# Where the streamed rows and the weight rings of a two-block forward pass begin, modulo 256 bytes

## The reference, cut to what matters

```python
# first block, x: (1, 256, 2048)
z = rms_norm(h, attn_norm_g) @ w_in                      # 2048 x 5120
h = h + concat(diff_attention(...), gmlp(...)) @ w_out    # 2048 x 2048
f = rms_norm(h, ffn_norm_g)
h = h + (silu(f @ ffn_w1) * (f @ ffn_w3)) @ ffn_w2        # 2048 x 5632, twice, and back
h = h + (p @ pl_w_up) * sigmoid(h @ pl_w_gate)
x = rms_norm(h, final_norm_g)
# second block, 16 meta tokens ahead of the 256
proj = rms_norm(h, norm_mix_g) @ w_in                     # 2048 x 12288
h = h + (g_a * (pool(u) @ pool_w) * pool_scale + g_b * ((gb * conv(gc * v)) @ conv_out_w)) @ w_o
gate, up = split(rms_norm(h, norm_ffn_g) @ w_gate_up)     # 2048 x 11264
h = h + (silu(gate) * up) @ w_down
out = rms_norm(h, norm_final_g)[:, 16:]
```

## Time and profile before

| | |
|---|---|
| median of three runs | 2665.52 us |
| the profiled execution, its own time | 2665.68 us |
| its span, first to last instruction | 2663.6 us |
| TensorE busy | 2652.8 us, 15711 matmuls |
| VectorE busy | 1658.5 us |
| ScalarE busy | 1236.0 us |
| mean granted TensorE clock | 0.999 |

### The profile page before, as it was taken

The page is one execution under the profiler, slowest core; times in us unless marked ns, Lnnn a source line. Parts: engine busy times, 40 slices in busy tenths (PEclk is TensorE's granted clock), DMA queues, the critical chain, the costliest instruction groups (busy, mean ns, idle before and its releaser), DMA issues.

```text
span 2663.6 us, 39872 instructions
## 1 busy us (share of the span) xinstructions
PE 2652.8 (100%) x15711; PEld 2347.5 (88%) x15711; DVE 1658.5 (62%) x1645; ACT 1236.0 (46%) x1355; POOL 0.8 (0%) x7
## 2 busy tenths in 40 slices
PE   9999999999999999999999999999999999999998
PEld 8889888888888888888999999888888888888887
DVE  6567766555565556795676666556765645564555
ACT  5456554444444444565443443444554434443444
POOL 0000000000000000000000000000000000000000
PEclk9999999999999999999999999999999999999999
DMA  8554555655656555555555555555565555565553
GB/s 291 184 174 145 195 189 193 193 193 188 198 181 205 181 199 189 185 191 191 176 175 189 181 184 182 190 182 190 189 205 189 189 189 189 189 198 192 180 192 138
DMA packets 254251, 502.92 MB, mean 189 GB/s; under 512 B 8130, under 2 KB 11652, under 8 KB 253988
## 3 DMA queue, kind: packets, MB, share of 16 engines
q1 hardware_dynamic: 252180, 497.61, 56.6%
q10 hardware_dynamic: 1952, 3.68, 0.4%
HBM read 498.37 MB, written 2.88 MB: 188 GB/s over the span
## 4 chain that ended last, share of the span: by engine, by line
PE 99%; DVE 0%; ACT 0%; DMA 0%; issue 0%; ACTq 0%; DVEq 0%
PE ps L1359 49%; PE ps L1373 24%; PE ps L1392 4%; PE ps L1394 4%; PE ps L1393 4%; PE ps L1412 4%; PE ps L1411 4%; PE ps L1410 3%; PE ps L1403 0%; PE ps L1402 0%; PE ps L1404 0%; PE ps L1322 0%; DMA xtok<-in_x_dram 0%; PE ps L1547 0%; PE ps L1545 0%; PE ps L1546 0%
## 5 line engine op out<-in xcount | busy, mean ns | idle before, releaser
L825 DVE TENSOR_TENSOR lo<-raw,hi 128x1024 fp32r<-128x1024 f32 x940 | 1127.8, 1223 | 852.2 <-ACT hi L491 843.6
L491 ACT ACTIVATE hi<-raw 128x1024 fp32r<-128x1024 f32 x940 | 971.5, 1055 | 1061.2 <-PE ps L1373 483.6
L1359 PE MATMUL ps<-A,hi 128*128 128x512 f32 x3648 | 862.8, 393 | 0.0
L1359 PEld LDWEIGHTS ps<-A,hi 128*128 128x128 f32 x3648 | 675.6, 188 | 140.4
L1359 PE MATMUL ps<-B,hi 128*128 128x512 f32 x1984 | 477.5, 394 | 0.0
L1373 PEld LDWEIGHTS ps<-A,lo 128*128 128x128 f32 x3648 | 438.0, 188 | 12.0
L1373 PE MATMUL ps<-A,lo 128*128 128x256 f32 x3648 | 439.9, 277 | 0.0
L1359 PEld LDWEIGHTS ps<-B,hi 128*128 128x128 f32 x1984 | 365.3, 188 | 74.8
L1373 PEld LDWEIGHTS ps<-B,lo 128*128 128x128 f32 x1984 | 246.1, 188 | 10.0
L1373 PE MATMUL ps<-B,lo 128*128 128x256 f32 x1984 | 247.8, 279 | 0.0
L1412 PE MATMUL ps<-B,lo 128*128 128x258 f32 (+1 forms) x768 | 219.4, 286 | 0.0
(11 more groups left out here) (240 smaller groups left out, 1342.6 us busy)
## 6 DMA issues: line engine op xcount, KB each, us to landing
raw<-in_w_in_dram SPq DMA_DIRECT2D x136, 1024.0 KB, 5.1
raw<-in_ffn_w_dram SPq DMA_DIRECT2D x132, 1024.0 KB, 5.1
raw<-in_w_gate_up_dram SPq DMA_DIRECT2D x88, 1024.0 KB, 5.0
raw<-in_w_down_dram SPq DMA_DIRECT2D x44, 1024.0 KB, 5.1
raw<-in_w_out_dram SPq DMA_DIRECT2D x16, 1024.0 KB, 5.2
raw<-in_pl_w_gate_dram SPq DMA_DIRECT2D x16, 1024.0 KB, 5.1
raw<-in_conv_out_w_dram SPq DMA_DIRECT2D x16, 1024.0 KB, 5.1
raw<-in_w_o_dram SPq DMA_DIRECT2D x16, 1024.0 KB, 5.1
```

The lines of the kernel that those rows point to most:

```text
L491: act.activation(hi[:, slot % RING], raw[:, raw_slot, 2 * (slot % 2):2 * (slot % 2) + 2, :], ACT.Copy).then_inc(hi_ready, 1)
L825: dve.tensor_tensor(lo[:, slot % RING], raw[:, slot // 2 % RAWS, 2 * (slot % 2):2 * (slot % 2) + 2, :], hi[:, slot % RING], ALU.subtract). ...
L1359: last = pe.matmul(ps[:, b0 + m, :], high(slot, kk, m), both, start=j == 0 and kk == 0, stop=ends and j == seg.pieces - 1 and kk == 1)
```

## The change

It moves where buffers begin and touches nothing else: the instructions of each engine, their order, their shapes and their waits stay the same; only addresses differ. `ln_stats` has 24 columns instead of 32 (the code uses 24). The places of `ln_stats`, `rstd_meta`, `r_row`, `vec1` and `vec2` in the order of allocation change, and so the starts of the big buffers. `B_token` goes; what used it uses `B_halves`.

Starts modulo 256 bytes:

| buffer or view | before | after |
|---|---|---|
| raw | 128 | 128 |
| hi | 128 | 128 |
| lo | 0 | 192 |
| A | 192 | 128 |
| B | 128 | 64 |
| B_halves | 192 | 128 |
| B_token | 64 | gone |
| h, pb_copy, work | 128 | 64 |
| PT (the operand of segment plup) | 224 | 192 |

Start of the streamed operand minus start of the stationary tile that is loaded beside it, modulo 256 (192 is 64 below):

| segments and pass | before | after |
|---|---|---|
| halves, high pass (row against hi) | 64 | 0 |
| halves, low pass (row against lo) | 192 | 192 |
| token, v and g: hi, lo, hi against the row of A | 192, 64, 192 | 0, 64, 0 |
| token, f2_down: hi, lo, hi against the row of B | 64, 192, 64 | 0, 64, 0 |
| wide: high parts, low parts, high parts | 0, 192, 0 | 192, 192, 192 |
| conv: the same | 56, 192, 56 | 248, 192, 248 |

```diff
-TOKEN_AT = META + 32
...
         hi = sb("hi", [P, RING, 2, GC], F32R)
-        ln_stats = sb("ln_stats", [P, 32])
+        rstd_meta = sb("rstd_meta", [P, META])
         lo = sb("lo", [P, RING, 2, GC], F32R)
 
         tiny = sb("tiny", [P, 2, TM])
-        rstd_meta = sb("rstd_meta", [P, META])
+        r_row = sb("r_row", [P, TM])
         A = sb("A", [P, KT, 2 * T], F32R)
-        r_row = sb("r_row", [P, TM])
-        vec2 = sb("vec2", [P, V2N])
+        ln_stats = sb("ln_stats", [P, 24])
+        vec1 = sb("vec1", [P, V1K])
...
-        vec1 = sb("vec1", [P, V1K])
+        vec2 = sb("vec2", [P, V2N])
...
-        B_token = B[:, :, TOKEN_AT:TOKEN_AT + 2 * T]
...
-                                evacuate(kind, G, end, b0, turn * len(seg.kinds) + g, first_tile(seg, turn, g), more,
-                                         B_token if seg.name.startswith("f2") else B_halves)
+                                evacuate(kind, G, end, b0, turn * len(seg.kinds) + g, first_tile(seg, turn, g), more)
...
-                    given.mark(act.activation(some(A if kind == "cb" else to_b, k, 4, 0, T), work[:, :, :], ACT.Copy))
+                    given.mark(act.activation(some(A if kind == "cb" else B_halves, k, 4, 0, T), work[:, :, :], ACT.Copy))
...
-                    finish_split(to_b if kind == "up" else A, k)
+                    finish_split(B_halves if kind == "up" else A, k)
...
-                return {"A": A, "B": {"halves": B_halves, "token": B_token}.get(layout, B), "PT": PT}[buf]
+                return {"A": A, "B": B_halves if layout in ("halves", "token") else B, "PT": PT}[buf]
...
-                            Xh, Xl = B_token[:, k, a * P:(a + 1) * P], B_token[:, k, T + a * P:T + (a + 1) * P]
+                            Xh, Xl = B_halves[:, k, a * P:(a + 1) * P], B_halves[:, k, T + a * P:T + (a + 1) * P]
```

More of the change, by code:

```diff
@@ L522, in residual_out, with evacuate @@
                 ready.skip()
-            def evacuate(kind, G, end, b0, gi, k, more, to_b):
+            def evacuate(kind, G, end, b0, gi, k, more):
                 if kind == "cg":
```

## The result

The changed kernel takes 2669.43 us (median of 20 runs, 2669.33 to 2670.11) against 2665.43 us for the kernel before on the same chip (20 runs, 2665.07 to 2666.12). The ratio is 1.0015, with a 95% interval of 1.0009 to 1.0021. The prediction said 2652 us.

The account below looks back on a forecast made before the run. The prediction took TensorE's cost per matmul as the bound, with no engine holding it up and full clock. From 2665.7 us it took 13.4 for quick cadence throughout halves, nothing for the rest: 2652.3, predicted as 2652 us, range 2634 to 2700.

Parts of the forecast that it names:

- What bounds the kernel: Whole kernel: TensorE, busy 2652.8 of 2663.6 us, is not held up and has full clock; one matmul's cost remains.
- Relations alone count: Halves low pass: if only relations matter, its relation stays 192 and its cost changes only by its cadence.
- Edits at nothing: Small ScalarE and VectorE buffers change place; a few per cent slowdown would be covered by 843.6 and 483.6 us of waiting.
- the choice of the cadence: Halves segments, both passes: quick cadence throughout, -13.4 us, giving 2652 us; chance 0.35.
- the two cadences: Halves matmuls: quick, 229.1 ns high and 113.4 low; slow, about 234 and 118; about a quarter of work slow.
- a high pass at neither 229 nor 234: Sign in halves bursts that the relation sets the excess itself and the two cadences are the wrong frame.
- The argument of the smaller jump: Halves, switch from high to low: relation moves by 64 instead of 128, which should disturb a quick rhythm less.
- rival three: Halves high pass itself gets cheaper, -19.8 us, with quick cadence -13.4 and perhaps token 6.9; 2626 to 2640 us, chance 0.11.
- rival one: Slow cadence locks in for halves, wholly or in part; +34.8 us if all slow; 2671 to 2700 us, chance 0.34.
- The rival that addresses don't matter: Whole kernel: start addresses have no effect, or gains and losses offset; 2665.5 us, chance 0.20.
- Token segments: v, g and f2_down, 384 and 1056 matmuls: relations may explain 0.7 ns, 1.0 us either way; taken as 0.
- Wide and conv: 2304 matmuls, relation 0 or 56 becomes 192 or 248: 1.6 us either way; taken as 0.

Follow-up runs that it names:

- f3: Against the changed kernel, the last high tile before a low burst in halves segments is streamed as two matmuls, cut at 384 columns; 2660.34 us.
- e1 to e7: Seven runs changing only the places of buffers, each measured against the kernel before; 2669.50 to 2682.76 us.
- e11: The changed kernel with segments gbr, cout and wo in alternating order (longer bursts); 2669.69 us.
- e6: Against the kernel before, only buffer places change: rows at 64, both rings at 128, high and low relations both 192; 2674.71 us.
- e7: Against the kernel before, only buffer places change: rows 0, high ring 128, low ring 64, relations high 128, low 192; 2672.91 us.
- f5 to f7: f3 with gbr, cout and wo in alternating order, cut at 384, 320 and 288 columns; 2658.85, 2654.28 and 2650.70 us.
- e9: The kernel before with segments gbr, cout and wo alone in alternating order, bursts of 32 instead of 16; 2660.79 us.
- e8: The kernel before with segments plgate, ga, gbr, cout and wo in alternating order, bursts of 32 instead of 16; 2668.29 us.

## Why the prediction was wrong

*What bounds the kernel* was right. TensorE's own gaps made nearly the whole difference (3.8 us), and waits, clock and the other engines stood as before.

*Relations alone count* was half right. Absolute starts don't matter for what was tried: e3 moved hi, lo, `A` and `B` by 128 bytes and changed 0.1 us. But relations alone don't fix the gap; how a burst is entered does as much (f3). The rule of the Trainium skill that I had weighed ("TensorE: Matmul & The Clock Gate", step-by-step part: two independent read ports, no bandwidth taken by the next load) would have made e1 to e7 equal. They spread from 2669.5 to 2682.8 us, so the trace disagrees with it as far as these float32 streams at full rate go.

*Edits at nothing* held: ScalarE and VectorE were busy 1235.9 and 1657.8 us, as before within 1 us.

*The failed step* is the choice of the cadence: "A smaller jump should disturb a quick rhythm less ... I choose: quick throughout, -13.4 us." The choice was to bring -13.4 us; halves work as a whole went up by 2.8 us (-13.8 in the high pass, +16.6 in the low pass). It was wrong in its premise, that the two cadences of before would stay the two that there are, and that both passes would be quick or slow together. At relation 0 the high pass has a rhythm of its own: after about five matmuls it settles at 226.7 ns, below both 229 and 234. The prediction had named this sign ("a high pass at neither 229 nor 234"), and it came. That rhythm leads to the 117.8 ns cadence of the low pass, whatever the length of the burst (e11). The quick low pass, two thirds of the low matmuls before, went to next to none. The argument of the smaller jump fails too: from the high to the low relation it is 0 in e6 and 64 in e7, with quick low passes (113.7 and 114.6 ns on average), and 64 in the changed kernel, with slow ones (117.9). "The low pass of halves keeps its relation, ... its cost changes only by which cadence it is in" was true and was worth +16.6 us; I had put all of the cadence on the favourable side. Why the settled high pass of relation 0 leads to the slow low pass is not known; f3 and f5 to f7 show only that a shorter last stream before the low burst undoes it.

The rivals had parts of it. The high pass did get cheaper (rival three had 3.5 ns below 229.1; 1.9 came in a burst of 32, 1.3 on average), and the slow cadence did lock in (rival one, but for the low pass only, and I had sized it with the high pass in it, +34.8 us). The result is their sum, 0.15%: within the bound of no change, in the range, and not the likeliest case. That the range held it says little, since it spanned both signs. The rival that addresses don't matter named the right size for the wrong reason; its "gains in one segment offset by losses in another" is near to what happened, between passes rather than segments.

Token segments: I took 0 with a bound of 1.0 us. They cost 2.0 us. The rows showed relations (192, 64, 192) and (64, 192, 64), neither of which has the 0 that the changed kernel has in its high passes; the bound from two near values was too tight. Wide and conv at 0, bound 1.6 us: measured -0.9.

## What to carry to other kernels

When TensorE never waits and its clock is full, read the time from start to start of equal matmuls. If equal instructions show two values, the gain may lie in how the stream and the next load fall together, and a burst's price then depends on how it was entered. Such a layout can't be judged by one pass: measure the pair, since here every layout with the cheap high pass had the dear low pass. And a hand-over can be changed for a few nanoseconds by cutting one matmul in two. At the 211 hand-overs of f3 that was worth 9.1 us, more than going back to the best of the eight layouts (4.0).

## What the runs showed of the hardware

- Float32 matmuls with a load beside each take 213.3 ns of columns and 226.7 to 233.8 ns from start to start (512 columns), and 106.7 and 113.3 to 120.1 ns (256 columns), by the relation of the two reads modulo 256 bytes and by how the burst was entered.
- The rhythm of the high pass at relation 64 repeats over three matmuls (226, 229, 232 ns). At the addresses of before, all 110 quick high bursts of 32 led to a quick low burst; of 14 quick ones of 16, nine led to a slow one, so the length weighs but doesn't decide alone. All 87 slow high bursts led to slow low ones.
- A wait can end the quick cadence, and need not: the first wait in e9's cout cost the next two bursts their quick cadence, while behind the wait in e8's cout (the low burst from 1777.03) the high burst goes at 7.33/32 = 229.1 ns.
